# Rotations placed between the products for v and q, and differential attention read from PSUM with POOL scaling the second map, on one core

## The reference, cut to what matters

```python
def diff_attend(q, k, v, lam):
    s = jnp.einsum('bqhcd,bkhcd->bhcqk', q, k) * (q.shape[-1] ** -0.5)
    p = jax.nn.softmax(s.astype(jnp.float32), axis=-1)
    a = (p[:, :, 0] - lam * p[:, :, 1]).astype(v.dtype)
    return jnp.einsum('bhqk,bkhd->bqhd', a, v)

kb_all = jnp.concatenate([_da_qk(kbc), rope_2d(_da_qk(kb), tabs)], axis=1)
yb = diff_head_norm(diff_attn_blocks(rope_2d(_da_qk(qb), tabs), kb_all, vb_all, lam), ...)
```

## Time and profile before

| what | value |
|---|---|
| median of 3 runs | 4822.42 us (4822.33 to 4823.9) |
| the profiled execution's own time | 4819.14 us |
| its span in the trace | 4817.4 us |
| mean granted clock of PE | 0.964 of full speed |
| PE / DVE / ACT / POOL busy | 4411.8 / 1426.8 / 1002.2 / 100.0 us |

### The profile page before, as it was taken

One profiled execution on the slowest core, in us unless ns is written; L12 is line 12 of the kernel. 1 busy time (PEld: TensorE's weight loads), 2 busy tenths in 40 slices (PEclk: granted clock), 3 DMA queues, 4 the chain that ended last, 5 costly groups with the idle time before them and its releaser, 6 DMA issues. The chain is left out here.

```text
span 4817.4 us, 62989 instructions
## 1 busy us (share of the span) xinstructions
PE 4411.8 (92%) x28228; PEld 2722.9 (57%) x28228; DVE 1426.8 (30%) x2148; ACT 1002.2 (21%) x1817; POOL 100.0 (2%) x87
## 2 busy tenths in 40 slices
PE   7999999999999789988999689999899989969887
PEld 6888799677888545545555433333345454433333
DVE  1585744422230221336211210111214171120112
ACT  2113422201110311425111211111314051121111
POOL 0000022000000000000000000000000000000000
PEclk9999999899999999999999889999999999989999
DMA  2583200222222211010111379888211102159996
GB/s 81 201 283 112 67 4 4 77 74 79 70 76 60 61 35 59 23 35 1 53 53 53 131 295 353 312 330 319 70 47 47 53 1 87 70 207 427 427 427 256
DMA packets 187942, 652.82 MB, mean 136 GB/s; under 512 B 10934, under 2 KB 75126, under 8 KB 163110
## 3 DMA queue, kind: packets, MB, share of 16 engines
q1 hardware_dynamic: 184038, 635.09, 35.2%
q0 software_dynamic: 3648, 13.88, 0.9%
HBM read 635.71 MB, written 11.67 MB: 134 GB/s over the span
## 5 line engine op out<-in xcount | busy, mean ns | idle before, releaser
L326 PE MATMUL psum<-arena 128*128 128x264 f32 (+5 forms) x7520 | 2139.3, 446 | 56.7 <-ACT arena L996 19.2
L326 PEld LDWEIGHTS psum<-arena 128*128 128x128 f32 (+1 forms) x7520 | 1433.8, 192 | 745.7 <-issue 322.4
L908 PE MATMUL psum<-arena 128*64 128x512 f32 x3072 | 701.0, 603 | 49.2 <-DMA arena<-in_w_e 44.8
L908 PEld LDWEIGHTS psum<-arena 128*64 128x64 f32 x3072 | 213.1, 138 | 476.7 <-issue 426.6
L1902 PE MATMUL psum<-arena 64*64 64x64 f32 x7488 | 227.8, 219 | 9.6 <-issue 4.5
L651 PE MATMUL psum<-arena 128*128 128x512 f32 x544 | 234.4, 592 | 0.0
L1902 PEld LDWEIGHTS psum<-arena 64*64 64x64 f32 x7488 | 225.9, 135 | 12.3 <-issue 7.7
L1591 DVE SCALAR_TENSOR_TENSOR arena<-psum,arena 128x512 f32<-128x512 f32 (+1 forms) x160 | 110.7, 697 | 379.0 <-PE psum L888 372.1
L1575 DVE TENSOR_TENSOR arena<-arena,psum 128x512 f32<-128x512 f32 x32 | 22.0, 687 | 612.3 <-PE psum L914 330.7
L914 PE MATMUL psum<-arena 128*32 128x256 f32 x3072 | 185.7, 382 | 0.0
L651 PEld LDWEIGHTS psum<-arena 128*128 128x128 f32 x544 | 103.4, 190 | 129.5 <-issue 128.7
(11 more groups left out here) (314 smaller groups left out, 3392.5 us busy)
## 6 DMA issues: line engine op xcount, KB each, us to landing
arena<-in_w_e SPq DMA_DIRECT2D x192, 2048.0 KB, 14.4
arena<-in_w_in SPq DMA_DIRECT2D x38, 2048.0 KB, 7.9
arena<-in_w_ada SPq DMA_DIRECT2D x24, 2048.0 KB, 8.7
arena<-in_ffn_up SPq DMA_DIRECT2D x22, 1024.0 KB, 7.6
arena<-in_w_branch SPq DMA_DIRECT2D x6, 2048.0 KB, 7.7
arena<-in_ffn_down SPq DMA_DIRECT2D x8, 1408.0 KB, 7.0
arena<-in_w_in SPq DMA_DIRECT2D x16, 512.0 KB, 4.4
arena<-in_w_out SPq DMA_DIRECT2D x4, 2048.0 KB, 7.9
```

Of the source, the lines that this page charges most:

```text
L326: mm = pe.matmul(PS[0:m, 2 * region + c, 0:cn], w[0:kp, k, j * P:j * P + m], rhs(k, c0, cn), start=(k == 0), stop=(k == s.kt - 1))
L908: mm = pe.matmul(PS[c * HD:c * HD + HD, b + (m > 0), :], x(kk), w[:, k, c * BW:c * BW + BW], start=(kk == 0), stop=(kk == KT - 1))
```

## The change

- The 8 rotations are taken out from behind the products. The 4 of k follow the first 4 token tiles of the product for v, those of q follow the product tiles for q, one tile late; the eighth comes behind the product. DVE's temporaries move from `SCR` to behind the sines in the `H` area.
- The scale of 1/8 moves from the score copies to the evacuation of q.
- The exponential for lambda moves ahead of the evacuation of kb on ACT.
- Scores of a map are two matmuls of 384 columns into two banks (one of 256 for a context unit); DVE takes the maximum and ACT the exponential straight from PSUM. The next unit's scores of a map wait for this unit's exponential of it.
- PE's order in a turn is: scores of map 0 of unit n, transposes of n - 2, scores of map 1 of n, product of n - 3.
- POOL scales map 1 (`da_x1`), DVE inverts both sums in one instruction and subtracts.
- ACT copies all six transposed tiles in one instruction; DVE's copy of two is gone.

The diff, without the removed `attend` and `counts` functions on ACT and DVE:

```diff
         for h in range(DA_H):
-            for q in q_ctx + [CTX + n * P for n in range(SEQ // P)]:
-                own = q < CTX
-                maps = []
-                for p0 in (0, HD):
-                    row = lambda o, c, n: A[p0:p0 + HD, o + h * T2 + c:o + h * T2 + c + n]
-                    maps.append((row(QR, q, P), row(KR, 0, CTX), None if own else row(KR, CTX, SEQ)))
-                da.append(dict(maps=maps, nk=2 if own else 6, v=lambda t, h=h: at(VR + t * BW + h * P, P), m=P,
-                               p0=0, out=at(YB + h * T2 + q, P)))
+            da += [(h, True, q) for q in q_ctx] + [(h, False, CTX + n * P) for n in range(SEQ // P)]
...
-        DA_S = lambda j: SCR + j % 6 * T2
+        DA_S = lambda n, m: SCR + (n % 3 * 2 + m) * T2
+        DA_KEYS = lambda n: CTX if da[n][1] else T2
...
-            def by_token(name, tiles, columns=False):
+            def by_token(name, tiles, columns=False, beside=None):
...
+                    if beside:
+                        beside(n)
...
+            def differences():
+
+                def scores(n, m):
+                    h, own, q = da[n]
+                    wt(pe, "rope_done", 5 + h)
+                    if n == 2:
+                        wt(pe, "rope_t", 8)
+                    if n:
+                        wt(pe, "da_e", 2 * n - 1 + m)
+                    r = slice(m * HD, m * HD + HD)
+                    query = A[r, QR + h * T2 + q:QR + h * T2 + q + P]
+                    for c in range(1 if own else 2):
+                        cn = CTX if own else T2 // 2
+                        keys = A[r, KR + h * T2 + c * cn:KR + h * T2 + c * cn + cn]
+                        mm = pe.matmul(PS[:, 2 * m + c, 0:cn], query, keys, start=True, stop=True)
+                    inc(mm, "da_s")
+
+                def turn(n):
+                    wt(pe, "da_p", n + 1)
+                    if n:
+                        wt(pe, "da_pt", n)
+                    for t in range(DA_KEYS(n) // P):
+                        tr = pe.transpose(PS[:, 4 + t // 4, t % 4 * P:t % 4 * P + P], at(DA_S(n, 0) + t * P, P), ident)
+                    inc(tr, "da_t")
+
+                def gather(n):
+                    h = da[n][0]
+                    wt(pe, "da_pt", n + 1)
+                    if n >= 2:
+                        wt(pe, "da_out", n - 1)
+                    nk = DA_KEYS(n) // P
+                    for t in range(nk):
+                        mm = pe.matmul(PS[:, 6 + n % 2, 0:P], at(VR + t * BW + h * P, P), at(DA_P(n) + t * P, P),
+                                       start=(t == 0), stop=(t == nk - 1))
+                    inc(mm, "da_o")
+
+                for n in range(len(da) + 3):
+                    if n < len(da):
+                        scores(n, 0)
+                    if 2 <= n < len(da) + 2:
+                        turn(n - 2)
+                    if n < len(da):
+                        scores(n, 1)
                     if n >= 3:
-                        wt(pe, f"{a}_pt0", n - 2)
-                        if seq_units[n - 3]:
-                            wt(pe, f"{a}_pt1", seq_units[n - 3])
-                    if 2 <= n <= n_u + 1:
-                        u = units[n - 2]
-                        src = s_at((n - 2) * len(u["maps"]))
-                        wt(pe, f"{a}_p", n - 1)
-                        for t in range(u["nk"]):
-                            tr = pe.transpose(PS[:, 4 + t // 4, t % 4 * P:t % 4 * P + P], at(src + t * P, P), ident)
-                            if t == min(3, u["nk"] - 1):
-                                inc(tr, f"{a}_t0")
-                        if u["nk"] > 4:
-                            inc(tr, f"{a}_t1")
-                    if n >= 3:
-                        u = units[n - 3]
-                        if n >= 5:
-                            wt(pe, f"{a}_out", n - 4)
-                        for t in range(u["nk"]):
-                            mm = pe.matmul(PS[u["p0"]:u["p0"] + u["m"], 6 + n % 2, 0:P], u["v"](t),
-                                           at(p_at(n - 3) + t * P, P), start=(t == 0), stop=(t == u["nk"] - 1))
-                        inc(mm, f"{a}_o")
+                        gather(n - 3)
...
             pe.wait_ge(*taken(f"qa{l}"))
             neighbours()
             wt(pe, "na_out", len(na))
             products(pe, f"kb{l}", rhs)
-            by_token(f"vb{l}", range(T2 // P))
-            products(pe, f"qb{l}", rhs)
-
-            pe.wait_ge(*taken(f"qb{l}"))
-            for n in range(8):
+
+            def rotate(n):
+                name, i = ("kb", n) if n < 4 else ("qb", n - 4)
+                pe.wait_ge(*taken(f"{name}{l}", i + 1))
                 if n >= 4:
                     wt(pe, "rope_t", n - 3)
-                r = (KR if n < 4 else QR) + n % 4 * T2 + CTX
-                inc(pe.matmul(PS[:, 4 + n % 4, :], sb(ROT, P), at(r, SEQ), start=True, stop=True), "rope_r")
-            wt(pe, "rope_done", 8)
-            attend(da, "da", DA_S, DA_P)
+                r = (KR if n < 4 else QR) + i * T2 + CTX
+                inc(pe.matmul(PS[:, 4 + i, :], sb(ROT, P), at(r, SEQ), start=True, stop=True), "rope_r")
+            by_token(f"vb{l}", range(T2 // P), beside=lambda n: rotate(n) if n < 4 else None)
+            products(pe, f"qb{l}", rhs, beside=lambda t: rotate(3 + t) if t else None)
+            rotate(7)
+            differences()
...
+            def differences():
+
+                def power(n, m):
+                    wt(act, "da_max", 2 * n + m + 1)
+                    if n >= 3:
+                        wt(act, "da_t", n - 2)
+                    x = at(DA_S(n, m), DA_KEYS(n))
+                    src = PS[:, 2 * m, 0:CTX] if da[n][1] else PS[:, 2 * m:2 * m + 2, 0:T2 // 2]
+                    inc(nc.scalar.activation(x if da[n][1] else spread(x, 2), src, ACT.Exp, bias=at(cell(n, 0) + m, 1),
+                                             accum_out=at(cell(n, 1) + m, 1)), "da_e")
+
+                def take_turned(n):
+                    wt(act, "da_t", n + 1)
+                    if n >= 2:
+                        wt(act, "da_o", n - 1)
+                    inc(nc.scalar.activation(at(DA_P(n), DA_KEYS(n)),
+                                             PS[:, 4:6, :].rearrange("p b t -> p (b t)")[:, 0:DA_KEYS(n)], ACT.Copy), "da_pt")
+
+                def take_out(n):
+                    h, _, q = da[n]
+                    wt(act, "da_o", n + 1)
+                    inc(nc.scalar.activation(at(YB + h * T2 + q, P), PS[:, 6 + n % 2, 0:P], ACT.Copy), "da_out")
+
+                for n in range(len(da) + 4):
+                    if n < len(da):
+                        power(n, 0)
+                    if 2 <= n < len(da) + 2:
+                        take_turned(n - 2)
+                    if n < len(da):
+                        power(n, 1)
                     if n >= 4:
+                        take_out(n - 4)
...
             neighbours()
+            wt(act, "lam_dot", 1)
+            inc(nc.scalar.activation(at(LAMS, 2), at(LAMS, 2), ACT.Exp), "lam_exp")
             take(act, f"kb{l}", k_at(KR))
             take(act, f"vb{l}", v_at)
-            take(act, f"qb{l}", q_at(QR))
-            wt(act, "lam_dot", 1)
-            inc(nc.scalar.activation(at(LAMS, 2), at(LAMS, 2), ACT.Exp), "lam_exp")
-            attend(da, "da", DA_S, DA_P, DA_SCALE, 6)
+            take(act, f"qb{l}", lambda i, acc, j: nc.scalar.activation(
+                spread(at(QR + q0 + i * T2, nq), nqc), acc, ACT.Copy, scale=ATT_SCALE))
+            differences()
...
+            for n in range(len(da)):
+                x1 = at(DA_S(n, 1), DA_KEYS(n))
+                wt(pool, "da_r", n + 1)
+                inc(nc.gpsimd.tensor_scalar(x1, x1, at(cell(n, 2) + 1, 1), at(LAMC, 1), ALU.mult, ALU.mult), "da_x1")
...
+            def differences():
+
+                def largest(n, m):
+                    wt(dve, "da_s", 2 * n + m + 1)
+                    src = PS[:, 2 * m, 0:CTX] if da[n][1] else PS[:, 2 * m:2 * m + 2, 0:T2 // 2]
+                    inc(V.tensor_reduce(at(cell(n, 0) + m, 1), src, AX.X if da[n][1] else AX.XY, ALU.max, negate=True), "da_max")
+
+                def inverse(n):
+                    wt(dve, "da_e", 2 * n + 2)
+                    inc(V.reciprocal(at(cell(n, 2), 2), at(cell(n, 1), 2)), "da_r")
+
+                def normal(n):
+                    x, x1 = (at(DA_S(n, m), DA_KEYS(n)) for m in range(2))
+                    wt(dve, "da_x1", n + 1)
+                    inc(V.scalar_tensor_tensor(out=x, in0=x, scalar=at(cell(n, 2), 1), in1=x1, op0=ALU.mult,
+                                               op1=ALU.subtract), "da_p")
+
+                for n in range(len(da) + 1):
+                    if n:
+                        inverse(n - 1)
+                    for m in range(2):
+                        if n < len(da):
+                            largest(n, m)
+                    if n:
+                        normal(n - 1)
...
```

(64 more changed lines are left out.)

82 lines of the change are left out of this document (removed).

## The result

The changed kernel takes **4847.7 us** (median of 5 runs, 4844.65 to 4851.78); the kernel before, in 5 runs beside it, 4823.9 us (4822.33 to 4825.06). The ratio is 1.005, 95% interval 1.0035 to 1.0065: 24 us slower, where 35 us of gain were forecast. The profiled execution took 4847.7 us with a span of 4845.9 us, 28.5 us over the span of before.

What follows compares the result with a forecast made beforehand. PE was taken to become attention's bound at 4.9 us per full unit. Gains of 17.8 us (rotations), 8.2 (layer 1) and 8.6 (layer 0) total 34.6, giving 4787 us, range 4768 to 4810.

Steps and rivals of the forecast that it cites:

- the clock term: Both attention stages: low clock at the start costs 4 us in layer 1 and 5 us in layer 0.
- The rotations: Between products and attention: 8.6 us in place of 17.5, 8.9 us gained per layer, 17.8 in both.
- PE as the bound: Full attention units: PE needs 4.9 us each and becomes the bound, instead of 5.4 to 5.6 us on DVE.
- The single buffer: Scores' PSUM: next unit's map waits for this unit's exponential, a 3.6 us loop, below PE's 4.9.
- POOL: Scaling of map 1 in attention: taken as 2.07 us, hidden; POOL bounds only from 3.5 us on.
- DVE and ACT: Per full unit: DVE 3.1 us, ScalarE 2.9 us, with operands read from PSUM; neither bounds.
- Lambda's exponential: Moved ahead of kb's products into ScalarE's idle time: 0.2 us, nothing waits.
- The slower case: Both attention stages: PE's low clock decides above 87 us low; 120 us low gives 4838; chance 0.04.
- POOL as the bound: Attention: POOL's scaling takes 4.15 us, period 5.6, some 15 us gain left, 4807; chance 0.10.
- attention gaining nothing through the buffer: Attention: single PSUM buffer bounds if PSUM reads cost 0.9 us more each; rotation alone pays, 4804; chance 0.06.
- The better case: Attention: short units at 1.75 us, no clock loss, POOL near 0.7 us give 4769; chance 0.20.

Runs made afterwards that it cites:

- b1: The changed kernel with dummy full-array 512-column matmuls behind the scores of unit 0 (four) and unit 1 (two); 4790.36 us, ratio 0.9934.
- a3: The changed kernel with both maps' scores next to each other on PE, ahead of the transposes; 4767.47 us, ratio 0.9891.
- a4: The changed kernel with every score matmul over all 128 rows instead of 64, which gives another output; 4768.81 us, ratio 0.9889.
- a1: The kernel before with only the rotations moved among the products, and what they need; 4797.33 us, ratio 0.9951.
- a2: The changed kernel with its rotations put back behind the product for q, so the new attention stands alone; 4833.79 us, ratio 1.0025.
- c1: The changed kernel with adjacent maps' scores, both exponentials ahead of the transposed copy, and dummy matmuls at the start; 4756.56 us, ratio 0.9859.
- c3: The changed kernel with dummy matmuls at the start and PE made to wait for POOL's scaling before scores of units 8 and 9; 4811.83 us, ratio 0.9968.
- b3: The changed kernel with adjacent maps' scores and both exponentials of a unit ahead of ACT's transposed copy; 4761.54 us, ratio 0.9875.
- c2: The changed kernel with six dummy full-array 512-column matmuls once, behind unit 5, and none at the start; 4830.53 us, ratio 1.0016.

## Why the prediction was wrong

**The step that failed is the clock term**, "8 us at the low level lose 4" in layer 1 and "5 for the clock" in layer 0. Measured were 92.2 and 54.6 us low. What they cost is read from b1, the same order without low time: its stretches are 40.4 and 22.8 us shorter than the changed kernel's, together 63 us in place of 9 (half of all the low time would be 73, but a part of it was idle). With this term and the two smaller ones below the forecast's own sum closes: 4787 - 9 + 63.3 for the clock, + 10.7 for PE's units, - 3.4 for the rotations, makes 4848.6; the median is 4847.7. The assumption behind the 8 us was that the clock comes up when transposes and products join the scores, since in the earlier trace rows it was 1.00 with PE busy for two thirds of the time. That row had map 0 and map 1 side by side on both halves of the array. The change takes the maps apart, and a3 and a4 show that this is what counts once the clock has fallen. The forecast saw that the order ends the overlap and priced it in columns alone, 1.3 against 2.8 us.

**The rest of the sum held within 12 us.** At full clock the forecast is 4787 - 9 = 4778, and b1, the same order at full clock with its filler, takes 4790.4. (The last step of the sum rounds down: 4784.5 + 3.3 is 4787.8.)
- The rotations: 10.6 us gained a layer for 8.9. In a1 the attention stretches (117.4 and 93.8 us) are as long as before or 1 us shorter, so a1's 26 us are 21 from the rotations and a few from what follows. When the scores began DVE had the rest of the seventh rotation and all of the eighth before it, 3.1 us, not 2.0, but PE's 1.57 us of scores hid part of it.
- PE as the bound: yes, without a wait for 70 us on end. Its unit at full clock is 5.31 us, not 4.9: scores take 1.48 a map, not 1.4, the transposes 0.81, not 0.68, the product 1.53, not 1.43. At that size a full unit is no faster than before's 5.4, so at full clock most of the gain is the rotations and the low time that is gone. Over 15 units the 0.4 us make 6; b1's stretch is 89.1 against the 82.8 forecast at full clock, while layer 0's 108.0 stands against 103.6; 10.7 us together.
- The single buffer: hidden from unit 2 on as forecast (PE's waits for the exponential end with the one of 1.28 us). That it bounds units 0 and 1 was in the sum too (as a gain of 2.8 us), but not what those waits, 3.56 and 1.28 us, do to the clock.
- POOL: 0.98 us, not 2.07, and hidden. The Trainium skill, "GPSIMD Engine Reference", section "Engine selection", calls one-input operations roughly line-rate; 0.98 against DVE's 0.68 lies nearer to that than to the value taken. It moved nothing, as PE bounds.
- DVE and ACT: the forms read from PSUM cost what their rows said.
- Lambda's exponential: the forecast priced its move at nothing, and no wait for it shows, but it isn't free to stay where it was. DVE waits for it ahead of its rotations, so behind qb it would stand behind work that waits for those same rotations.

**The rivals.** The slower case named the mechanism, the place and the point from which it decides (87 us low), and gave 120 us low and 4838; 147 us and 4847.7 came. Its chance of 0.04 was too small: the row against it (1.00 with PE idle for a third) was of another kind of work, while the row for it, 9.54 us busy of 10.5 at 0.50, was of the same kind as the new stage's units 0 and 1 and was read as a matter of 8 us. POOL as the bound and attention gaining nothing through the buffer are refuted by the rows of the lines by form. The better case's time (4769) was reached in a3, but by another order of the scores, so this doesn't speak for its terms.

**What stays open.** Why the clock came up after some 55 us in layer 0 and 92 in layer 1 of the changed kernel, but after 41 and 48 in a2, with the same units in between; a2's even came up for some 3.5 us in layer 1, fell behind the 1.49 us wait and came up again. a2's long idle stretch in the rotations lies ahead of both stages; no run here varied that alone. Why a wait of 1.5 to 1.8 us is followed by a fall in a2 and c1 and not in c3's profile is open too.

## What to carry to other kernels

When a change makes PE the bound, price its time at the lower clock first: read the granted clock beside each busy share, ask which rows of the array the work uses and whether PE idles just ahead of it, and treat both levels as states that can last. Matmuls on different halves of the array's rows belong next to each other in program order, with the buffers they wait for released together; here the order of the scores alone (a3) turned 0.5% slower into 1.1% faster, and the release (b3) added 6 us. If the start of such a stage can't be freed of waits, a few dummy full-array matmuls in them are cheap.

## What was not expected of the hardware

- A PE busy for 100% of 70 us at a granted clock of 0.50, and one burst of full-array matmuls, 6.3 us of PE (c2), that lifts it for the rest of the stage. The Trainium skill, "TensorE: Matmul & The Clock Gate", section "A second HAM failure mode: psum-queue depth-cycling", tells of short idle times between groups of matmuls that make the clock alternate; in the changed kernel it did not alternate, it fell once in each layer and stayed down, without idle time. The kernel before does alternate, in layer 0: windows of 4 us from 2148 on are granted 1.00, 0.70, 0.87 and 1.00, with PE waits of 1.0 to 1.7 us among them.
- Score matmuls on 64 rows cost 1.48 us for four passes of 384 columns, the same on 128 rows 1.29 (a4): running alone they lose 0.19 us, some 0.05 us a pass.
- Matmuls on different row halves start out of program order, by the start marks of the records. The program issues map 0's 256 keys (L757), map 0's 512 (L759), then map 1's 256 (L757) and 512. On PE's timeline of the kernel before, a unit of layer 1:

```profile
3923.41 0.78 PE L757 MATMUL psum<-arena 64*128 64x256 f32 x4
3923.94 0.59 PE L759 MATMUL psum<-arena 64*128 64x512 f32 x1
```

All four L757 passes, map 1's two among them, start before the first L759 pass, which stands ahead of map 1's in the program. The prediction cited the Trainium skill, "TensorE: Matmul & The Clock Gate", section "The mechanism", for all matmuls keeping program order; across row halves these rows say otherwise, and the sentence that nothing reorders the work doesn't hold for them. In the rows of the changed kernel nothing of map 1 ran ahead of the full-array transposes.
